# Six weight slots for three in the experts, and half a remainder on GpSimd

## The reference

```
def hier_moe(x, wg, bg, we, be, w1, w3, w2):
    # top-1 of 4 groups, then top-2 of the 8 experts in the group: (token, expert, gate)
    ...
    def expert_block(args):
        xe, e = args                      # 128 tokens of one expert
        hid = jax.nn.silu(xe @ w1[e]) * (xe @ w3[e])
        return hid @ w2[e]
    ...
    # out = for each token the sum of its two experts' rows, each times its gate
```

## Time and profile before

| | |
|---|---|
| time, median of 3 runs | 2533.58 us (2531.31 to 2536.4) |
| span of the profiled execution | 2540.5 us |
| experts of layer 0, span time | 757 to 1345 us |
| experts of layer 1, span time | 1921 to 2504 us, then one further block to the end |
| busy: PE, DVE, ACT, POOL | 95%, 73%, 57%, 19% |

### The profile page before, as it was taken

One profiled execution on the slowest core, in us unless ns is written; L12 is line 12 of the kernel. 1 busy time (PEld: TensorE's weight loads), 2 busy tenths in 40 slices (PEclk: granted clock), 3 DMA queues, 4 the chain that ended last, 5 costly groups with the idle time before them and its releaser, 6 DMA issues. The chain is left out here.

```text
span 2540.5 us, 32760 instructions
## 1 busy us (share of the span) xinstructions
PE 2408.3 (95%) x11718; PEld 1969.6 (78%) x11718; DVE 1845.3 (73%) x2212; ACT 1458.0 (57%) x1784; POOL 484.1 (19%) x429
## 2 busy tenths in 40 slices
PE   8989999899999999999997999997998999999997
PEld 7768877577877888888886877875887888888884
DVE  7748855668479888899883141478678889988983
ACT  6338843323127788788874241267426788877872
POOL 0001100101002333243320000036001433322321
PEclk9999999989989999999998999999998999999999
DMA  5110002210348999999994032022428999999997
GB/s 183 34 68 1 2 16 71 75 34 13 125 150 316 379 375 396 366 393 386 381 377 132 11 117 82 34 51 94 151 99 314 361 368 382 380 369 373 400 382 265
DMA packets 95674, 540.20 MB, mean 213 GB/s; under 512 B 19405, under 2 KB 31278, under 8 KB 70487
## 3 DMA queue, kind: packets, MB, share of 16 engines
q1 hardware_dynamic: 73830, 499.76, 50.7%
q0 software_dynamic: 19008, 33.61, 5.4%
q10 hardware_dynamic: 2736, 5.51, 0.6%
HBM read 519.37 MB, written 55.08 MB: 226 GB/s over the span
## 5 line engine op out<-in xcount | busy, mean ns | idle before, releaser
L2456 DVE TENSOR_TENSOR wL_rest<-ring,wH 128x2048 fp32r<-128x2048 f32 x384 | 869.5, 2288 | 122.4 <-ACT wH L2387 116.9
L2387 ACT CAST wH<-ring 128x2048 fp32r<-128x2048 f32 x384 | 731.1, 1911 | 183.8 <-DMA ring<-in_moe_w 167.2
L2251 PE MATMUL psum<-wH,xgH 128*128 128x512 f32 x1024 | 406.5, 397 | 13.2 <-DVE xgL L2456 13.1
L2253 PE MATMUL psum<-wH,xgL 128*128 128x512 f32 x1024 | 399.3, 390 | 0.0
L2259 PE MATMUL psum<-wL_rest,xgH 128*128 128x512 f32 x1024 | 274.5, 390 | 0.0
L2251 PEld LDWEIGHTS psum<-wH,xgH 128*128 128x128 f32 x1024 | 192.4, 188 | 56.9 <-issue 10.2
L2259 PEld LDWEIGHTS psum<-wL_rest,xgH 128*128 128x128 f32 x1024 | 192.2, 188 | 40.3
L2253 PEld LDWEIGHTS psum<-wH,xgL 128*128 128x128 f32 x1024 | 192.7, 188 | 37.8
L2251 PE MATMUL psum<-wH,hidH 128*128 128x512 f32 x512 | 207.3, 405 | 3.9 <-DVE hidL L2456 3.9
L2253 PE MATMUL psum<-wH,hidL 128*128 128x512 f32 x512 | 201.4, 393 | 0.0
L2168 POOL COPY gidx<-slots 128x1 int32 (+1 forms) x60 | 65.1, 1085 | 470.5 <-PE psum L2268 470.5
(11 more groups left out here) (466 smaller groups left out, 4755.3 us busy)
## 6 DMA issues: line engine op xcount, KB each, us to landing
ring<-in_moe_w SPq DMA_DIRECT2D x188, 2048.0 KB, 9.7
ring<-in_ev_w_in SPq DMA_DIRECT2D x6, 2048.0 KB, 8.4
ring<-in_od_w_in SPq DMA_DIRECT2D x6, 2048.0 KB, 8.8
ring<-in_moe_w SPq DMA_DIRECT2D x16, 512.0 KB, 7.9
xnT<-in_moe_w SPq DMA_DIRECT2D x4, 2048.0 KB, 13.2
xn_scratch<-xn_route SPq DMA_DIRECT2D x14, 512.0 KB, 2.6
v_att<-in_x SPq DMA_DIRECT2D x8, 512.0 KB, 4.7
ring<-in_ev_w_out SPq DMA_DIRECT2D x2, 2048.0 KB, 7.8
```

The lines of the kernel that those rows point to most:

```text
L2251: nc.tensor.matmul(psum[:, bank, :], xh[:, k, :], w3[0][:, n, cols], start=(half == 0 and n == 0), stop=False)
L2253: nc.tensor.matmul(psum[:, bank, :], xl[:, k, :], w3[0][:, n, cols], start=False, stop=False)
L2387: nc.scalar.copy(half_of(wH, b, e, c, half), raw(e, c, half)).then_inc(w_high, 1)
L2456: return nc.vector.tensor_tensor(out, whole, high.bitcast(F32), ALU.subtract)
```

## The change

Three things are changed in `experts`, and nothing else in the program:

- The weights go through six slots: the three of the ring, and the three of `w_over` (the halves of `xnT`, and `ow2`). The semaphores of the new slots are `room_in`. The first block's weights for a further block are now loaded when the slots 3, 4 and 5 are freed at the end. The loads that a later phase needs (L180 before) go out earlier by three matrices.
- For every expert but the first, the remainder of the second half of c=1 is made by GpSimd, between `fetch` and `give`. PE and SP wait for it on `pool_rest`. DVE leaves it out.
- The scratch of the extra lists moves out of `xnT` (now weights) into `y` and into a tile of its own. For this, `hit`, `cmp` and the first steps on `q` and `r` move from `over_part(0)` to `over_part(1)`, the reduction `eov` moves from part 3 to part 1, and ScalarE's `store_y` waits for the lists that use `y` (`gates_ok` 2 for expert 0, `over_listed` for expert 1).

```diff
+                def slot(i, b, c):
+                    if first(i, b):
+                        return c
+                    return (2, 3, 4)[c] if b else (5, 0, 1)[c]
...
+                def place(slot_n):
+                    return ring[:, (s0 + slot_n) % RING, :] if slot_n < RING else w_over[slot_n - RING]
...
+                def by_gpsimd(i, b, c, half):
+                    return c == 1 and half == 1 and not first(i, b)
...
+                def wait_rest(eng, i, b, c, half):
+                    if by_gpsimd(i, b, c, half):
+                        eng.wait_ge(pool_rest, 2 * i + b)
+                    else:
+                        eng.wait_ge(w_rest, rests(i, b, c, half))
...
                     def _(sp):
+                        def pair(i):
+                            freed(*((0, 0, 0) if one_pair(i) else (i - 1, 0, 1)))
+                            load(0, 2 * i, 1)
+                            freed(*((0, 0, 1) if one_pair(i) else (i - 1, 0, 2)))
+                            load(1, 2 * i - 1, 2)
+                            for c in range(2):
+                                freed(i - 1, 1, c)
+                                load(2 + c, 2 * i + 1, c)
+                            freed(i - 1, 1, 2)
+                            load(4, 2 * i, 2)
...
+                        load(3, 1, 1)
+                        sp.wait_ge(gates_listed, 1)
+                        load(4, 0, 2)
+                        load(5, 2, 0)
...
                         def first_block(n):
                             for c in range(3):
+                                freed(*((PAIRS - 1, 1, 1), (PAIRS - 1, 1, 2), (PAIRS, 0, 0))[c])
                                 sp.dma_start(w_over[c], expert_src(layer, e, c)).then_inc(w_in[c], 16)
...
                     def _(pool_e):
+                        def split(i, b):
+                            c, half = 1, 1
+                            pool_e.wait_ge(w_high, 2 * chunk(i, b, c) + half + 1)
+                            nc.gpsimd.tensor_tensor(half_of(wL, i, b, c, half), raw(i, b, c, half),
+                                                    half_of(wH, i, b, c, half).bitcast(F32), ALU.subtract
+                                                    ).then_inc(pool_rest, 1)
...
+                        with pool_e.Fori(4, PAIRS) as i:
+                            for b in range(2):
+                                fetch(i, b)
+                                split(i - 1, b)
+                                give(i - 2, b)
...
                     def _(pe):
-                            pe.wait_ge(w_rest, q + 1)
+                            wait_rest(pe, i, b, c, half)
...
                     def _(act):
+                            if first(i, b):
+                                act.wait_ge(gates_ok, 2)
+                            if second(i, b):
+                                act.wait_ge(over_listed, 1)
...
                     def _(dve):
+                        def split(i, b, c, half):
+                            if by_gpsimd(i, b, c, half):
+                                return
```

More of the change, by code:

```diff
@@ L51 @@
 OVERP = OVER + 1
+PAIRS = NE // 2
 EMPTY = 2048
@@ L2113, in load @@
                         def load(slot_n, e, c):
[L2114 to L2121, removed]
-                                load(slot(e, 0), 1, 1)
-                                freed(e, 1)
-                                load(slot(e, 1), 0, 2)
-                                return
-                            for c in range(3):
-                                freed(e, c)
-                                load(slot(e, c), (e if c == 2 else e + 1), c)
@@ L2296, in one, with gate @@
[L2296 to L2305 removed]
+                        def gate(i, b, c):
+                            if c == 0 and not first(i, b):
+                                pe.wait_ge(silu_ok, 2 * i + b)
+                            if c == 1 and not first(i, b):
+                                pe.wait_ge(hid_ok, 2 * i + b)
+                            for half in range(2):
+                                product((2 + c,), xgH, xgL, i, b, c, half, range(4 * half, 4 * half + 4))
@@ new lines, in out, with one @@
+                        def out(i, b, at_i, at_b, c):
+                            pe.wait_ge(hl_ok, 2 * i + b + 1)
+                            if not first(i, b):
+                                pe.wait_ge(y_moved, 2 * i + b)
+                            for half in range(2):
+                                product((5, 6), hidH, hidL, at_i, at_b, c, half, range(2 * half, 2 * half + 2))
+                        def one(i, b):
+                            pe.wait_ge(xl_ok, 2 * i + b + 1)
+                            gate(i, b, 0)
+                            if not first(i, b):
+                                turn_hid(*before(i, b))
+                            gate(i, b, 1)
+                            if not (isinstance(i, int) and 2 * i + b == LAST):
+                                turn_x(*((i + 1, 0) if b else (i, 1)))
+                            if not first(i, b):
+                                out(*before(i, b), i, b, 2)
@@ L2610, in moe @@
                 halves = xnT[:].rearrange("p k t -> p (k t)").rearrange("p (c n) -> p c n", c=2)
[L2611 to L2612 removed]
+                w = (halves[:, layer, :], halves[:, 1 - layer, :], w2[:])
+                experts(layer, lists, total, yidx, oidx, w)
         @phase
```

384 lines of the change are left out of this document (193 added, 191 removed).

## The result

The changed kernel takes 2567.8 us (2561.7 to 2569.5, 4 runs) where the kernel before takes 2535.0 on the same chip (2531.3 to 2536.8): 1.0122 of before, interval 1.0104 to 1.0139. The medians differ by 32.8 us; the ratio, which isn't that of the two medians, stands for 31 us. The forecast was 2545, 11 us slower than before, with a range to 2576. The sign is right, and the forecast rise is a third of the measured one.

What follows compares the result with a forecast made beforehand. PE's matmuls, 17.70 us per expert, were taken to bound the kernel. From the 2533.6 us median, -5.0 (slots) + 7.0 (steady cost) + 9.2 (first experts) gave 2544.8, forecast 2545; own range 2539 to 2551, whole range 2528 to 2576.

Steps and rivals of the forecast that it cites:

- What bounds the kernel: In both layers' experts, PE's matmuls at 17.70 us per expert set the end; stalls cost only 9.6 us in the profile.
- The slots, -5.0: In the experts, six slots remove all of PE's stalls for late weights: -5.0 us on the median, -9.6 on the profile.
- GpSimd's 4.54 us, and one after another: In each expert but the first, GpSimd's subtraction takes 4.54 us and runs in turn with DVE's remainders, adding 4.40.
- side by side: Rival: DVE and GpSimd really work at the same time in the experts; 2524 to 2531 us, say 2527; chance 0.18.
- The steady cost, +7.0: Over 27 steady experts per layer, the chain of DVE and GpSimd takes 17.83 us against PE's 17.70: +7.0 us.
- the chain fits: Rival: GpSimd needs 4.2 us or less, or partly overlaps `hidL`; no steady cost, 2538 us; chance 0.15.
- The first experts, +9.2: Before expert 2's tokens, GpSimd's turn, moved lists and `eov` lengthen DVE's chain and PE's wait: +4.6 us per layer.
- What GpSimd's subtraction costs in all: In the experts, its steady cost plus its share in the first experts: 7.0 + 2 x 2.2 = 11.4 us.
- The rest, at nothing: GpSimd's queue, ScalarE's new waits and SP's loads at the experts' end and for the next phase cost 0 us.
- The sum: Whole kernel, on the median: 2533.6 - 5.0 + 7.0 + 9.2 = 2544.8 us, forecast as 2545.
- GpSimd slower: Rival: GpSimd's subtraction in the experts is slower or kept waiting; 2576 us at 5.1 us, 2623 at 5.93; chance 0.13.
- All five signs: Experts' trace: subtraction 4.5 us, DVE's fifth remainder 4 or longer, distances 17.8 to 17.9, expert 2's wait near 6, ScalarE's near zero.

Runs made afterwards that it cites:

- e12: The kernel before, run once more with nothing changed for a second profile; 0.9995 of before, 2536.2 us.
- e11: e5 with the reduction `eov` made in part 0, before expert 1; 0.9991 of before, 2530.8 us.
- e7: The changed kernel, but GpSimd makes both halves of c=1 in each expert but the first, DVE the other four; 1.1150 of before, 2826.3 us.
- e9: e6, but GpSimd makes 1024 columns of its half and DVE the other 1024; 1.0040 of before, 2542.6 us.
- e6: The changed kernel, with SP waiting for both fetches of the first tokens before a layer's first expert weight load; 1.0067 of before, 2550.8 us.
- e1: The changed kernel, but DVE makes all six remainders of each expert and GpSimd none; 1.0044 of before, 2548.0 us.
- e2: The changed kernel with the first operations on the extra lists back in part 0, GpSimd's subtraction kept; 1.0116 of before, 2565.4 us.
- e4: e1 and e2 together: of the change only six slots and the place of `eov` are left; 1.0043 of before, 2545.9 us.
- e10: e5 with GpSimd's subtraction added from expert 2 on; 1.0063 of before, 2548.7 us.
- e5: e4, with SP waiting for both fetches of the first tokens before a layer's first expert weight load; 0.9989 of before, 2531.8 us.
- e3: The changed kernel, but GpSimd's first subtraction is that of expert 2 and DVE makes all six of expert 1; 1.0088 of before, 2558.2 us.
- e8: The kernel before, with its three slots and lists in place, and GpSimd's subtraction alone added; 1.0296 of before, 2604.8 us.

## Why the prediction was right or wrong, by its own steps

- **What bounds the kernel.** Right. PE at 17.70 us sets the period in every kernel with six slots and no long operation on GpSimd.
- **The slots, -5.0.** Right in mechanism, and by the traces in size: the stalls are gone in every six-slot kernel, and they were 5.5 us in e12. The times don't show it: e11 is 0.09% under before, 2.3 us, with an interval from -5.3 to +1.0.
- **GpSimd's 4.54 us, and one after another.** Right: 4.54 at 805.30, and e7 and the rows of e9 exclude that the two work side by side. The Trainium skill (GPSIMD Engine Reference, section 3.1) states 4497 ns for an addition of this size, which is as near. The prediction took that the turn of each costs the other its length; e7 shows that an engine can be kept out for longer.
- **The steady cost, +7.0.** Right in mechanism: 6.7 by the turned tokens, and about 7 us between e6 and e9, where this chain drops below PE's, with 1.2 us of shorter waits in it. The rival that the chain fits is out: it holds only in e9. That the size is so near is in part luck. The terms listed (11.0 + 2.4 + 4.40) add up to 17.80 and not to the 17.83 taken, which would be 5.4 us, and by them the cost is nothing up to 4.44 us of GpSimd and not 4.2. In the trace GpSimd took 4.49 us of the chain in place of 4.40.
- **The first experts, +9.2.** The mechanism is right, and the wait "near 6 us" came out at 5.69. The step that failed in size took the wait as the whole cost. Behind it PE runs at half clock for some microseconds, and the distance across it grew by 6.6 and 6.4 us: 13.0 in place of 9.2.
- **What GpSimd's subtraction costs in all.** Too low. In timed runs it is 18 to 20 us (the changed kernel against e1, e2 against e4) for 11.4, and 18 in e10 against e11 (1.2 of it `eov`), where 6.8 was expected. The traces show parts that the sum has no term for: half clock behind the wait for expert 2, and the wait at the end. They are not priced one by one.
- **The rest, at nothing.** This is the step that failed. Of SP's loads I costed those at the end of the experts and those for the next phase, and not those at their start, although the diff shows `load(3, 1, 1)` ahead of any wait. They are the first thing that six empty slots allow, and the tokens' fetch was in flight there. By e5 and e6 it costs 14 us, more than any term in the sum. The accumulating DMA behind GpSimd's last subtraction, also in this step, costs 0 to 2.6 us at the end; I had looked only at loads there.
- **The sum.** 2535.0 - 5.5 + 6.7 + 13.0 + 14 = 2563.2, and with the 2 us at the end 2565, against 2567.8 measured. By ratios: e6 to e5 is 0.78% or 20 us for GpSimd and the moved lists together (6.7 + 13.0, less what `eov` costs, which e5 has too), the fetch 14, the slots -3. That these add up to the 31 us of 1.0122 is no evidence, since the three ratios multiply to it whatever the causes are. That the traces give 6.7 + 13.0 and 13 us for nearly the same parts is. How the 20 us divide is less sure: by the waits some 5 us, 2 x (1.7 + 0.7), came with the moved lists and `eov`, while e2 gained 1.5 us, give or take 6.
- **The rivals.** The time fell between my forecast and "GpSimd slower", but by neither road: GpSimd was as fast as forecast. Without the late fetch the changed kernel is 2550.8 (e6), at the edge of my forecast's own range of 2539 to 2551. That 2567.8 lies within the whole range, 2528 to 2576, is luck: its upper part stood for a slower GpSimd, and was filled by a late fetch.
- **What would show it.** All five signs came as written: GpSimd's subtraction with 4.5 us or a little more, DVE's fifth remainder with over 4 us (5.7), distances of 17.8 to 17.9, the wait near 6, and ScalarE's wait for weights gone. They could be right while the time was 22 us off, because none looked at the start of a layer.

## What to carry to other kernels

When a change gives a loader more free slots, look first at the moment when all of them are empty: what it can issue there goes out beside every small, urgent transfer of that moment, and a wait that lets the small one go first cost nothing here and gave back 14 us. Two elementwise engines that exclude each other add up to one chain, so moving work from the faster to the slower lengthens it by the difference of their prices (4.40 for 2.20 us here), however idle the slower one looks. After summing waits, ask for each long one whether PE comes back from it at full clock.

## What the runs showed of the hardware that I had not expected

- An engine that waits for the other doesn't get the turn between two operations that follow each other back to back: DVE's remainder took 11.50 us beside two subtractions of 9.09 us together (e7), as GpSimd's copy took 6.47 beside three remainders. In e7 DVE's record even begins 0.25 us before GpSimd's. Of the pair of ports that the two share, the Trainium skill (SBUF — State Buffer, "SBUF: two separate sides") states that whichever starts first has it for its whole instruction; for a single operation the traces agree (5.74 us beside one). In e7 they don't, if one goes by where the records start, and of a queue of two it says nothing.
- After a wait of PE of 3.9 us and more there was a stretch of 3.4 or 6.8 us at half clock behind it (changed kernel, e1 to e3, e6, e9), after one of 2.2 to 2.3 us sometimes (layer 0 of e4, e5 and e10, layer 1 of none), after one of 3.28 us in layer 1 of e8 but not in layer 0, and after 1.5 or 1.63 us never in these profiles.
- GpSimd's first fetches moved nothing in the 3.5 us after their issue while SP's loads were in flight, one of 2 MB issued 0.6 us after the first fetch among them (changed kernel, layer 0), though in the kernel before they moved 0.23 MB in as long beside 1.27 MB of loads with smaller packets.
